# A two-layer hybrid model on one core: the order and the places of the first expert stage's weight loads

## The chip, the cores and the metric

The kernel runs on one core of a Trainium2 chip. The metric is the device time of one execution in microseconds; the time before is the median of three runs. TensorE (PE, with its weight load PEld), VectorE (DVE), ScalarE (ACT), GpSimd (POOL) and SyncE (SP) run their own instruction streams and meet at semaphores. Transfers from the device's memory run on 16 DMA engines; nearly all are issued by SyncE and go through one queue, in order.

## The reference

Two layers over T = 272 tokens (16 meta, 256 of the sequence) of width 1024. Layer 0 mixes with RWKV-7 and RG-LRU, layer 1 with gated linear attention. After each stands a mixture of experts: 32 experts in 4 groups, two chosen for each token.

```python
def hier_moe(h, w_group, b_group, w_router, b_router, w_gate, w_up, w_down):
    ...
    y = jnp.zeros_like(hf)
    for e in range(N_EXPERTS):
        hid = jax.nn.silu(hf @ w_gate[e]) * (hf @ w_up[e])
        y = y + (hid @ w_down[e]) * combine[:, e:e + 1]
    return y.reshape(B, T, D)
```

`w_gate` and `w_up` are 1024 x 256 for each expert and `w_down` is 256 x 1024, all float32: 1 MB for each matrix (here and below, 1 MB is 1024 KB), 96 MB for each layer. The part of RWKV that the text names: its output is centred head by head, scaled, gated and multiplied with the output weights.

```python
    mean = jnp.mean(o, axis=-1, keepdims=True)
    var = jnp.mean(jnp.square(o - mean), axis=-1, keepdims=True)
    o = ((o - mean) * lax.rsqrt(var + GN_EPS)).reshape(B, T, W) * ln_g.astype(f32) + ln_b.astype(f32)
```

## The kernel before, in words

Everything is written out by hand, in one program for each engine; the order of the work on an engine is the order of the lines.

**Expert stage.** `experts(y)` on TensorE goes through eight groups of four experts (q = 0 to 7). A group has three *units*, u = 3q (gate), 3q + 1 (up) and 3q + 2 (down), each of 4 MB. The tokens of each expert (at most 32) are gathered by matmuls into `xgT`, `half_gu` does gate and up (L1554, 64 matmul records of 32 x 256 for a unit), hid is turned (L1617), the down matmuls are L1630 (L1696 in the last group), and `combine` (L1512, L1514) brings the result back to the tokens. VectorE adds it to H (L2485, L2488). Between groups 3 and 4 there is a loop for experts with over 32 tokens (L1635 on), which makes one pass here.

**Places.** SBUF holds four slots of 4 MB, `slots[0]` to `slots[3]`, and `UNIT_SLOT` says which unit goes to which. In layer 0, units 0, 1, 2, 3, 4, 5 go to slots 1, 2, 3, 0, 1, 2, and unit 8 to slot 1 again. A slot may be filled once the unit before in it has been used (`wait_through`). The first units don't wait so long: parts of them have places of their own. `aside` holds the first halves (k = 0 to 3, 0.5 MB) of unit 4's up weights, for three of its four experts in layer 0; `apart` holds the first halves of unit 1's experts 1, 2 and 3. So a slot's half comes free while the other is in use, and `half_done` counts the halves used.

**Loads.** SyncE issues all of this in `experts(y)` at L348 to L486. The order around the change, for layer 0: unit 2 (down, slot 3, `whole`) after `sa_evac` 5 and `lru_in` 6; unit 0 (gate) after `oc_set` 5; unit 1 (up) after `mixE` 5, with two pieces set aside for unit 4; unit 3 (gate) and parts of unit 5 (down) after counts of `res_done` that say how much of the output projection is done; then the rest of units 4 and 5, and unit 8's halves ahead of units 6 and 7 at L441. `oc_set` is raised by VectorE for each of five chunks of the RWKV output at L2265, right after its centring; `sa_evac` is ScalarE's copy of a chunk's state, and `lru_in` 6 is the last step of the LRU (L2257). `loaded(u)` on TensorE waits for a unit's slot semaphore and, for the units in pieces, for a second one (`ld_pv_ys` for unit 1, `ld_wout` for 3, `ld_lruw_e5` for 5, `ld_u8_lastk` for 8); `ld_half` is for the pieces set aside.

**Small tiles.** `K1` holds the scan's reset mask and the GLA gate weights `gupO`; `m_lev` are masks of the RWKV stage; `wrr` are the raw router weights of both layers, turned into `wrc` by VectorE at L2303, which raises `wrc_set`. The router's scratch (`rt`) ends at column 37120 of M.

**Behind it.** Layer 1's projections (L1768, L1874), its attention, and `experts(1)`, whose loads begin at 522.30 us, when the attention's first output parts are done.

## Time and profile before

| | us |
|---|---|
| median of 3 runs | 782.89 |
| the three runs | 782.05, 782.89, 785.16 |
| span of the profiled execution | 778.7 |
| its own device time | not shown beside the runs |
| TensorE busy in the span | 718.9 (92%) |
| weight load busy | 459.4 (59%) |
| VectorE busy | 324.4 (42%) |
| mean rate of the DMA engines | 311 GB/s (242.14 MB) |
| chain that ended last: TensorE / DMA | 60% / 15% of the span |

The profile's times are from one execution, counted from its first instruction. Its own device time isn't among the numbers, so sums are made against its span. A wait is idle time of an engine and what ended it. "DMA to landing" is the time from the issue on SyncE to the last of the transfer's signals. The share of the DMA engines can come out slightly over 1.

### The profile page before, as it was taken

Reading aid. Unit: us, or ns where it says so; the run is one execution under the profiler, and the core shown is the slowest. Engines: PE = TensorE matmul, PEld = TensorE weight load, DVE = VectorE, ACT = ScalarE, POOL = GpSimd, SP = SyncE. Lnnn points to the kernel's source line nnn. Section 1 sums busy time; section 2 is a strip of 40 time slices with the busy share of each in tenths; the row PEclk is TensorE's granted clock in tenths of the full one; section 3 lists DMA queues with packets and bytes.
Section 4 is the critical chain, followed back from the end, with each engine's and each line's share of the span. In section 5 each row is a group of like instructions: output and inputs, shape, how many; then the busy total and the mean of one; then the engine's idle time right before and its main releaser. Section 6 shows DMA issues by size and latency. Waiting matters only on the chain.

```text
span 778.7 us, 16693 instructions
## 1 busy us (share of the span) xinstructions
PE 718.9 (92%) x7444; PEld 459.4 (59%) x7444; DVE 324.4 (42%) x688; ACT 205.9 (26%) x414; POOL 31.7 (4%) x99
## 2 busy tenths in 40 slices
PE   9999999999989998999999999999998976786696
PEld 7778787658646464564548746884764543343342
DVE  7476977535353422333235065541445321221222
ACT  2574577215100000000041454630510000000003
POOL 7006000000000000000000000000000000000000
PEclk9999999999999997999999999999999998989999
DMA  8644113499999999999999731019999999999995
GB/s 265 201 107 142 56 57 112 161 418 417 386 420 419 420 421 421 417 419 422 411 339 370 231 107 58 2 36 424 421 391 421 422 420 419 421 422 422 420 406 199
DMA packets 72757, 242.14 MB, mean 311 GB/s; under 512 B 9894, under 2 KB 37660, under 8 KB 52588
## 3 DMA queue, kind: packets, MB, share of 16 engines
q1 hardware_dynamic: 72476, 240.52, 79.0%
q8 instruction: 59, 0.97, 0.5%
q10 hardware_dynamic: 208, 0.54, 0.2%
q14 instruction: 14, 0.11, 0.0%
HBM read 240.00 MB, written 1.05 MB: 310 GB/s over the span
## 4 chain that ended last, share of the span: by engine, by line
PE 60%; DMA 15%; DVE 4%; issue 1%; SPq 1%; ACT 0%; ACTq 0%
PE ps L1554 11%; PE ps L1874 10%; PE ps L1396 7%; PE ps L1497 6%; DMA M<-in_m_w_gate_dram 6%; PE ps L1630 5%; PE ps L1512 5%; DMA M<-in_m_w_up_dram 4%; DMA M<-in_m_w_down_dram 4%; PE ps L1035 2%; DVE H L2488 1%; PE ps L1411 1%; PE ps L1696 1%; PE ps L1768 1%; PE ps L1505 1%
## 5 line engine op out<-in xcount | busy, mean ns | idle before, releaser
L1554 PE MATMUL ps<-M 128*32 128x256 f32 x2016 | 124.2, 396 | 18.4 <-DMA M<-in_m_w_gate_dram 11.4
L1554 PEld LDWEIGHTS ps<-M 128*32 128x32 f32 x2016 | 66.7, 114 | 74.7 <-issue 16.9
L1089 PE MATMUL ps<-M 128*128 128x272 f32 x352 | 85.3, 397 | 0.1
L1874 PE MATMUL ps<-M 128*128 128x256 f32 (+2 forms) x288 | 79.9, 434 | 0.0
L1497 PEld LDWEIGHTS ps<-M 128*128 128x128 f32 x608 | 71.5, 192 | 12.3 <-issue 11.8
L1497 PE MATMUL ps<-M 128*128 128x128 f32 x608 | 76.9, 278 | 0.0
L1089 PEld LDWEIGHTS ps<-M 128*128 128x128 f32 x352 | 65.6, 190 | 15.4 <-issue 1.7
L1630 PE MATMUL ps<-M 128*32 128x512 f32 x448 | 58.7, 671 | 15.5 <-DMA M<-in_m_w_down_dram 15.5
L1512 PE MATMUL ps<-M 128*128 128x512 f32 (+1 forms) x120 | 62.8, 647 | 5.3 <-DVE H L2488 5.3
L1874 PEld LDWEIGHTS ps<-M 128*128 128x128 f32 x288 | 53.7, 190 | 22.6 <-issue 15.6
L2485 DVE TENSOR_TENSOR H<-H,ps 128x512 f32<-128x512 f32 x60 | 41.2, 687 | 57.5 <-PE ps L1512 57.3
L1396 PE MATMUL ps<-M 128*128 128x512 f32 (+1 forms) x160 | 57.5, 512 | 0.0
L2464 DVE TENSOR_TENSOR M<-ps,gm 128x512 f32<-128x512 f32 x28 | 19.4, 692 | 59.7 <-PE ps L1497 59.7
L1512 PEld LDWEIGHTS ps<-M 128*128 128x128 f32 (+1 forms) x120 | 19.9, 194 | 40.7 <-DVE H L2485 18.1
L1630 PEld LDWEIGHTS ps<-M 128*32 128x32 f32 x448 | 15.7, 120 | 47.7 <-issue 46.5
L831 ACT ACTIVATE M<-ps 128x256 f32<-128x256 f32 x16 | 6.1, 383 | 140.7 <-PE ps L1554 140.7
L1396 PEld LDWEIGHTS ps<-M 128*128 128x128 f32 x160 | 29.6, 190 | 23.0 <-issue 21.5
L833 ACT ACTIVATE M<-ps 128x272 f32<-128x272 f32 x16 | 6.4, 397 | 127.1 <-PE ps L1505 127.1
L2540 DVE COPY M<-ps 128x512 f32<-128x512 f32 x14 | 9.7, 692 | 64.2 <-PE ps L1630 64.2
L839 ACT ACTIVATE M<-ps 128x512 f32<-128x512 f32 x16 | 9.6, 597 | 62.2 <-PE ps L1630 57.3
L2488 DVE TENSOR_TENSOR H<-H,ps 16x256 f32<-16x256 f32 x32 | 13.3, 414 | 29.7 <-PE ps L1514 29.4
L1021 POOL TENSOR_SCALAR M<-M,rs 128x512 f32<-128x512 f32 x1 | 1.6, 1566 | 548.0 <-DVE rs L1990 548.0
(462 smaller groups left out, 843.6 us busy)
## 6 DMA issues: line engine op xcount, KB each, us to landing
M<-in_m_w_gate_dram SPq DMA_DIRECT2D x31, 2048.0 KB, 19.0
M<-in_m_w_down_dram SPq DMA_DIRECT2D x24, 2048.0 KB, 22.8
M<-in_m_w_up_dram SPq DMA_DIRECT2D x24, 2048.0 KB, 21.6
M<-in_o_w_in_dram SPq DMA_DIRECT2D x12, 1024.0 KB, 9.5
M<-in_e_w_in_dram SPq DMA_DIRECT2D x11, 1024.0 KB, 6.7
M<-in_m_w_down_dram SPq DMA_DIRECT2D x10, 1024.0 KB, 18.1
M<-in_m_w_up_dram SPq DMA_DIRECT2D x9, 1024.0 KB, 17.9
M<-in_m_w_down_dram SPq DMA_DIRECT2D x4, 1536.0 KB, 13.3
```

Source lines behind the costliest of these rows:

```text
L1035: pe.matmul(ps[:, bank, :].rearrange("p (a c) -> p a c", a=4), ones[:, :], ones[:, :].unsqueeze(1).to_broadcast([P, 4, P]), start=True, st ...
L1089: ins = pe.matmul(ps[:, n % 4, 0:T], wringE[:, (n // 2) % 4, k, (n % 2) * P:(n % 2) * P + P], (xnE if n else xuE)[:, k], start=(k == 0), s ...
L1396: ins = pe.matmul(res, mixT[:, k, TOK[n]], w_out, start=(k == 0), stop=(k == 7))
L1497: ins = pe.matmul(ps[:, 1 + k // 4, (k % 4) * P:(k % 4) * P + P], xn[:, n, k, :], R[:, n, :], start=(n == 0), stop=(n == nt - 1))
L1512: return pe.matmul(ps[:, bank, :], rt_[:, TOK[n]], ys[:, 512 * hf:512 * hf + 512], start=True, stop=True)
L1554: ins = pe.matmul(ps[32 * e:32 * e + 32, 3 * x, 0:FF], xgT[q % 2][:, k, 32 * e:32 * e + 32], w, start=(k == 0), stop=(k == KD - 1))
L1630: ins = pe.matmul(ps[r, 4 + hf, :], hidT[:, k, r], dn_w[UNIT_SLOT[y][u]][:, e, k, 512 * hf:512 * hf + 512], start=(k == 0), stop=(k == 1))
L1874: ins = pe.matmul(ps[rows, unit % 4, 0:n], lhs(k), rhs(k), start=(k == 0), stop=(k == KD - 1))
L2464: return tt(xgT[q % 2][:, 4 * b:4 * b + 4], ps[:, 1 + b, :].rearrange("p (k t) -> p k t", k=4), gm[:, y, 4 * b:4 * b + 4].unsqueeze(2).to_ ...
L2485: return tt(H[:, n, c], H[:, n, c], ps[:, 6 + j % 2, :], ALU.add)
L2488: ins = tt(H[0:META, 2, c], H[0:META, 2, c], ps[32 * g:32 * g + META, 6 + j % 2, 0:256], ALU.add)
L2540: v.tensor_copy(yst[q % 2][:, 512:1024], ps[:, 5, :]).then_inc(s("yd"), 1)
```

## The change

1. `aside[0]` has a fourth place, at column 36096 of M: the first half of unit 4's expert 7 goes there as well (`set_aside(3)`), right behind unit 2. To make room, the router's scratch must end at 36096; `GE`, `DF`, `mR` and `mW` move to free columns below.
2. `apart[0]` is new: k = 0 to 2 of unit 1's expert 0, 0.375 MB, in `K1` at columns 1024 to 1792, sent after `wrc_set` 1. `K1` grows to 2112 columns and takes in `m_lev` and `wrr`, whose own tiles go.
3. Unit 2's first two experts are sent after the first `oc_set` instead of with the rest.
4. The place that (2) frees in slot 2 takes k = 0 to 2 of unit 5's expert 4, in the issues after `res_done` 5.
5. Unit 4's remaining halves go in two pieces of 1 MB after `half_done` 1. With slot 1's second halves no longer used by unit 4, all four second halves of unit 8 go after `gate_done` 1, ahead of unit 5's (before: three of them, behind unit 5's).
6. TensorE's `loaded(1)` waits for one transfer more, and `half_gu` reads the weights from the new places.

```diff
--- before.py
+++ after.py
@@ -108,14 +108,14 @@
         K0 = sb("K0", [P, 1056])
         m_ar = K0[:, 512:640].rearrange("p (x t) -> p x t", x=2)
         hsel, E2, cen, onesbd = K0[:, 640:672], K0[:, 672:800], K0[:, 800:928], K0[:, 928:1056]
-        K1 = sb("K1", [P, 1152])
+        K1 = sb("K1", [P, 2112])
         reset, gupO = K1[:, 0:640].bitcast(BF16), K1[:, 640:1152]
         ident = sb("ident", [P, P])
         ones = sb("ones", [P, P])
         id64 = sb("id64", [P, 64])
         before = sb("before", [P, P])
         iota = sb("iota", [P, P])
-        m_lev = sb("m_lev", [P, 6, L])
+        m_lev = K1[:, 1152:1536].rearrange("p (l t) -> p l t", l=6)
         pv = sb("pv", [P, NPV])
         gnT = sb("gnT", [P, 4, KD])
         gm = sb("gm", [P, 2, KD])
@@ -123,7 +123,7 @@
         omka = sb("omka", [P, 4])
         epsb = sb("epsb", [P, 2])
         dlast = sb("dlast", [P, 4, NC])
-        wrr = sb("wrr", [P, 2, KD, NG + NE])
+        wrr = K1[:, 1536:2112].rearrange("p (y k c) -> p y k c", y=2, k=KD)
         wrc = sb("wrc", [P, KD, NG + NE])
         BI = sb("BI", [P, 2, NG + NE])
         ss = sb("ss", [P, 5, 6])
@@ -277,16 +277,18 @@
         eg, ohg, sg4 = rt(3, NG), rt(3, NG), rt(3, NG)
         pe4 = rt(3, NG, 8)
         el, rk, A8, oh1, oh2, s8 = (rt(3, 8) for _ in range(6))
-        GE, DF = rt(3, 8, 8), rt(3, 8, 8)
+        GE, DF = at(28800, 3, 8, 8), at(28992, 3, 8, 8)
         AA = rt(48).bitcast(BF16).rearrange("p (t e) -> p t e", t=3)
         WT, RM = rt(3, NE), rt(3, NE)
         cnts, fl, pos, code = rt(NE), rt(2, NE), rt(64), rt(16)
         tab = rt(MAXOV + 1, 2)
-        tc2, mk, mR, mW, rme, wte = rt(2), rt(NE), rt(3, NE), rt(3, NE), rt(3), rt(3)
+        tc2, mk, rme, wte = rt(2), rt(NE), rt(3), rt(3)
+        mR, mW = at(29216, 3, NE), at(29312, 3, NE)
+        assert free[0] <= 36096
         level, cmp = at(31616, NE, 8), at(31616 + 8 * NE, 16, NE)
 
-        aside = [[K0[:, 0:D], K1[:, 0:D], yst[1]], [K0[:, 0:D], K1[:, 0:D], at(26624, D), yst[1]]]
-        apart = [None, xgT[1].rearrange("p k t -> p (k t)"), at(33792, D), yst[0]]
+        aside = [[K0[:, 0:D], K1[:, 0:D], yst[1], at(36096, D)], [K0[:, 0:D], K1[:, 0:D], at(26624, D), yst[1]]]
+        apart = [K1[:, 1024:1024 + 3 * FF], xgT[1].rearrange("p k t -> p (k t)"), at(33792, D), yst[0]]
         fnb = H[:, 2, :]
         fin = at(D, 2, D)
         ROOT_BANK = [1, 5]
@@ -364,15 +366,18 @@
 
                 def but_quarters(u, src, rest):
                     j = UNIT_SLOT[y][u]
-                    sp.dma_start(slots[j][:, 0, :], src[:, 0, :]).then_inc(s(f"ld_s{j}"), 16)
+                    sp.dma_start(slots[j][:, 0, 3 * FF:2 * D], src[:, 0, 3 * FF:2 * D]).then_inc(s(f"ld_s{j}"), 16)
                     sp.dma_start(slots[j][:, 1:3, D:2 * D], src[:, 1:3, D:2 * D]).then_inc(s(f"ld_s{j}"), 16)
                     sp.dma_start(slots[j][:, 3, D:2 * D], src[:, 3, D:2 * D]).then_inc(s(rest), 16)
                     sp.dma_start(apart[2], src[:, 2, 0:D]).then_inc(s(rest), 16)
 
                 if y == 0:
+                    sp.wait_ge(s("oc_set"), 1)
+                    sp.dma_start(slots[3][:, 0:2, :], down[:, 0:2, :]).then_inc(s("ld_s3"), 16)
                     sp.wait_ge(s("sa_evac"), NC)
                     sp.wait_ge(s("lru_in"), 6)
-                    whole(2, down[:, 0:4])
+                    sp.dma_start(slots[3][:, 2:4, :], down[:, 2:4, :]).then_inc(s("ld_s3"), 16)
+                    set_aside(3)
 
                 for u in range(NU):
                     q, kind = divmod(u, 3)
@@ -384,6 +389,8 @@
                         but_quarters(u, up[:, 0:4], "ld_pv_ys")
                         for e in range(2):
                             set_aside(e)
+                        sp.wait_ge(s("wrc_set"), 1)
+                        sp.dma_start(apart[0], up[:, 0, 0:3 * FF]).then_inc(s("ld_pv_ys"), 16)
                         continue
                     if u == 3 and y == 1:
                         for e in range(3):
@@ -402,6 +409,7 @@
                             sp.wait_ge(s("res_done"), 5)
                             sp.dma_start(slots[j][:, 2, :], gate[:, 6, :]).then_inc(s("ld_wout"), 16)
                             sp.dma_start(slots[UNIT_SLOT[y][5]][:, 1:4, 0:D], down[:, 5:8, 0:D]).then_inc(s("ld_lruw_e5"), 16)
+                            sp.dma_start(slots[UNIT_SLOT[y][5]][:, 0, 0:3 * FF], down[:, 4, 0:3 * FF]).then_inc(s("ld_lruw_e5"), 16)
                             sp.wait_ge(s("res_done"), 6)
                             sp.dma_start(apart[3], up[:, 3, 0:D]).then_inc(s("ld_pv_ys"), 16)
                             sp.dma_start(slots[j][:, 3, :], gate[:, 7, :]).then_inc(s(f"ld_s{j}"), 16)
@@ -420,10 +428,10 @@
                             set_aside(3)
                         if y == 0:
                             sp.wait_ge(s("half_done"), 1)
-                            sp.dma_start(slots[j][:, 3, 0:D], up[:, 7, 0:D]).then_inc(s("ld_half"), 16)
-                            sp.dma_start(slots[j][:, 0:3, 0:D], up[:, 4:7, D:2 * D]).then_inc(s(f"ld_s{j}"), 16)
+                            for e in (0, 2):
+                                sp.dma_start(slots[j][:, e:e + 2, 0:D], up[:, 4 + e:6 + e, D:2 * D]).then_inc(s(f"ld_s{j}"), 16)
                             wait_through(UNIT_PREV[y][u])
-                            sp.dma_start(slots[j][:, 3, D:2 * D], up[:, 7, D:2 * D]).then_inc(s(f"ld_s{j}"), 16)
+                            sp.dma_start(slots[UNIT_SLOT[y][8]][:, :, D:2 * D], down[:, 8:12, D:2 * D]).then_inc(s("ld_u8_lastk"), 16)
                             continue
                         else:
                             sp.wait_ge(s("half_done"), 3)
@@ -434,15 +442,13 @@
                     src = (gate, up, down)[kind]
                     if y == 0 and u == 5:
                         sp.wait_ge(s("half_done"), 2)
-                        sp.dma_start(slots[j][:, 0, 0:D], down[:, 4, 0:D]).then_inc(s(f"ld_s{j}"), 16)
+                        sp.dma_start(slots[j][:, 0, 3 * FF:D], down[:, 4, 3 * FF:D]).then_inc(s(f"ld_s{j}"), 16)
                         wait_through(UNIT_PREV[y][u])
-                        sp.dma_start(slots[j][:, 0:3, D:2 * D], down[:, 4:7, D:2 * D]).then_inc(s(f"ld_s{j}"), 16)
-                        sp.dma_start(slots[j][:, 3, D:2 * D], down[:, 7, D:2 * D]).then_inc(s("ld_lruw_e5"), 16)
-                        sp.dma_start(slots[UNIT_SLOT[y][8]][:, 0:3, D:2 * D], down[:, 8:11, D:2 * D]).then_inc(s("ld_u8_lastk"), 16)
+                        sp.dma_start(slots[j][:, :, D:2 * D], down[:, 4:8, D:2 * D]).then_inc(s(f"ld_s{j}"), 16)
                         continue
                     if y == 0 and u == 8:
-                        sp.dma_start(slots[j][:, 0:3, 0:D], down[:, 8:11, 0:D]).then_inc(s(f"ld_s{j}"), 16)
-                        sp.dma_start(slots[j][:, 3, :], down[:, 11, :]).then_inc(s(f"ld_s{j}"), 16)
+                        for e in (0, 2):
+                            sp.dma_start(slots[j][:, e:e + 2, 0:D], down[:, 8 + e:10 + e, 0:D]).then_inc(s(f"ld_s{j}"), 16)
                         continue
                     for h in range(1 if u == 3 else 0, 2):
                         if u == NU - 1:
@@ -1529,7 +1535,7 @@
                     j = UNIT_SLOT[y][u]
                     pe.wait_ge(s(f"ld_s{j}"), 32 * (FIRST_LAYER[j] * y + UNIT_TURN[y][u] + 1))
                     if y == 0 and u == 1:
-                        pe.wait_ge(s("ld_pv_ys"), 304)
+                        pe.wait_ge(s("ld_pv_ys"), 320)
                     elif y == 0 and u == 3:
                         pe.wait_ge(s("ld_wout"), 80)
                     elif y == 0 and u == 5:
@@ -1547,9 +1553,9 @@
                             w = gu_w[UNIT_SLOT[y][u]][:, e, k, :]
                             if u == 4 and k < KD // 2 and e < len(aside[y]):
                                 w = aside[y][e][:, FF * k:FF * k + FF]
-                            elif u == 4 and k >= KD // 2 and (e < 3 or y == 1):
+                            elif u == 4 and k >= KD // 2:
                                 w = gu_w[UNIT_SLOT[y][u]][:, e, k - KD // 2, :]
-                            elif u == 1 and y == 0 and k < KD // 2 and e:
+                            elif u == 1 and y == 0 and k < KD // 2 and (e or k < 3):
                                 w = apart[e][:, FF * k:FF * k + FF]
                             ins = pe.matmul(ps[32 * e:32 * e + 32, 3 * x, 0:FF], xgT[q % 2][:, k, 32 * e:32 * e + 32], w,
                                             start=(k == 0), stop=(k == KD - 1))
```

SyncE's stream from the first load of the expert stage on. The names are destination and source; `M` and `K` are the tiles M and K0 or K1. Before:

```order
L363 DMA M<-in_m_w_down_dram 128x2x2048 [waits lru_in,sa_evac]
L363 DMA M<-in_m_w_down_dram 128x2x2048
L468 DMA M<-in_m_w_gate_dram 128x2x2048 [waits oc_set]
L468 DMA M<-in_m_w_gate_dram 128x2x2048
L367 DMA M<-in_m_w_up_dram 128x2048 [waits mixE]
L368 DMA M<-in_m_w_up_dram 128x2x1024
L369 DMA M<-in_m_w_up_dram 128x1024
L370 DMA M<-in_m_w_up_dram 128x1024
L354 DMA K<-in_m_w_up_dram 128x1024 x2
```

and with the change:

```order
L376 DMA M<-in_m_w_down_dram 128x2x2048 [waits oc_set]
L379 DMA M<-in_m_w_down_dram 128x2x2048 [waits lru_in,sa_evac]
L356 DMA M<-in_m_w_up_dram 128x1024
L474 DMA M<-in_m_w_gate_dram 128x2x2048 [waits oc_set]
L474 DMA M<-in_m_w_gate_dram 128x2x2048
L369 DMA M<-in_m_w_up_dram 128x1280 [waits mixE]
L370 DMA M<-in_m_w_up_dram 128x2x1024
L371 DMA M<-in_m_w_up_dram 128x1024
L372 DMA M<-in_m_w_up_dram 128x1024
L356 DMA K<-in_m_w_up_dram 128x1024 x2
L393 DMA K<-in_m_w_up_dram 128x768 [waits wrc_set]
```

The first two experts of unit 2 stand under the first `oc_set`, a piece of up weights comes ahead of the gate loads, unit 1's first piece is shorter, and the rest of it stands last, under `wrc_set`.

SyncE's stream from unit 1's last piece (experts' half after `lg_done`) to the first load of unit 6. Before:

```order
L410 DMA M<-in_m_w_up_dram 128x1024 [waits lg_done]
L423 DMA M<-in_m_w_up_dram 128x1024 [waits half_done]
L424 DMA M<-in_m_w_up_dram 128x3x1024
L426 DMA M<-in_m_w_up_dram 128x1024 [waits gate_done]
L437 DMA M<-in_m_w_down_dram 128x1024 [waits half_done]
L439 DMA M<-in_m_w_down_dram 128x3x1024 [waits up_done]
L440 DMA M<-in_m_w_down_dram 128x1024
L441 DMA M<-in_m_w_down_dram 128x3x1024
L468 DMA M<-in_m_w_gate_dram 128x2x2048 [waits dn_done]
```

and with the change:

```order
L418 DMA M<-in_m_w_up_dram 128x1024 [waits lg_done]
L432 DMA M<-in_m_w_up_dram 128x2x1024 [waits half_done]
L432 DMA M<-in_m_w_up_dram 128x2x1024
L434 DMA M<-in_m_w_down_dram 128x4x1024 [waits gate_done]
L445 DMA M<-in_m_w_down_dram 128x256 [waits half_done]
L447 DMA M<-in_m_w_down_dram 128x4x1024 [waits up_done]
L474 DMA M<-in_m_w_gate_dram 128x2x2048 [waits dn_done]
L474 DMA M<-in_m_w_gate_dram 128x2x2048
```

Unit 4's remaining halves are two pieces, unit 8's four second halves stand right behind them under `gate_done`, and unit 5 has two loads left, one of 0.125 MB and one of 2 MB.

## Rows read from the trace of the kernel before

**Rows 1.** Waits of TensorE, 150 to 410 us: waiter, awaited, total us, times, longest.

```profile
PE ps L1512 <- DVE H L2488: 5.3, 7, 0.8
```

**Rows 2.** The same view, 600 to 760 us.

```profile
PE ps L1630 <- DMA M<-in_m_w_down_dram: 15.5, 4, 4.3
```

**Rows 3.** Busy times by stretch: PE, PEld, DVE, ACT, POOL, clock, DMA share, GB/s.

```profile
131.00:147.00 16.00, 14.83 (x538) 12.78 (x536) 14.33 (x28) 8.06 (x24) 0.00 (x0) 1.00 0.02 4
196.00:199.00 3.00, 2.93 (x49) 1.79 (x52) 2.57 (x13) 0.07 (x1) 0.00 (x0) 1.00 0.90 283
210.00:379.00 169.00, 158.69 (x1536) 93.01 (x1535) 60.57 (x121) 12.13 (x28) 0.53 (x1) 0.97 1.01 420
379.00:403.00 24.00, 22.77 (x203) 10.31 (x205) 7.72 (x14) 5.17 (x12) 0.00 (x0) 1.00 1.03 375
602.00:738.00 136.00, 103.78 (x1006) 55.97 (x1003) 30.05 (x50) 8.21 (x19) 0.00 (x0) 0.92 1.01 421
```

**Rows 4.** Issues and landings of L468 and L452, layer 0's group 7.

```profile
L468 SPq DMA_DIRECT2D M<-in_m_w_gate_dram x2: 367/420/472, 360.7 to 361.1; - x2
...
DMA to landing us min/median/max: 15.1/17.3/19.6
...
L452 SPq DMA_DIRECT2D M<-in_m_w_down_dram x4: 2985/4900/5281, 372.1 to 387.3; - x4
...
DMA to landing us min/median/max: 15.1/18.3/21.2
```

**Rows 5.** Timelines of weight load (PEld) and TensorE (PE): start, us, then the instructions.

```profile
198.37 3.21 PEld L1554 LDWEIGHTS ps<-M 128*32 128x32 f32 x64 [0.30 <-issue]
...
230.36 3.64 PE L1630 MATMUL ps<-M 128*32 128x512 f32 x32
...
245.68 3.18 PEld L1554 LDWEIGHTS ps<-M 128*32 128x32 f32 x64 [0.76 <-issue]
...
303.32 5.49 PE L1512 MATMUL ps<-M 32*128 32x512 f32 x6 [0.77 <-DVE H L2488]
...
317.51 3.03 PE L1512 MATMUL ps<-M 128*128 128x512 f32 x6 [0.76 <-DVE H L2488]
...
381.38 3.18 PEld L1554 LDWEIGHTS ps<-M 128*32 128x32 f32 x64 [0.76 <-DMA M<-in_m_w_gate_dram]
...
402.80 1.45 PEld L1696 LDWEIGHTS ps<-M 128*32 128x32 f32 x32 [0.17 <-issue]
```

**Rows 6.** Issues and landings of five lines, 146 to 203 us.

```profile
L363 SPq DMA_DIRECT2D M<-in_m_w_down_dram x1: 368/368/368, 146.6 to 146.6; - x1
...
DMA to landing us min/median/max: 9.0/9.0/9.0
...
L468 SPq DMA_DIRECT2D M<-in_m_w_gate_dram x2: 368/495/622, 147.9 to 148.3; - x2
...
DMA to landing us min/median/max: 17.7/19.9/22.2
...
L354 SPq DMA_DIRECT2D K<-in_m_w_up_dram x2: 432/740/1047, 160.7 to 161.1; - x2
L354 SPq DMA_DIRECT2D M<-in_m_w_up_dram x1: 432/432/432, 186.3 to 186.3; - x1
...
DMA to landing us min/median/max: 10.7/18.1/19.6
...
L440 SPq DMA_DIRECT2D M<-in_m_w_down_dram x1: 628/628/628, 202.5 to 202.5; - x1
...
DMA to landing us min/median/max: 9.8/9.8/9.8
```

**Rows 7.** Timeline of VectorE, first centring and router weights.

```profile
132.31 0.43 DVE L2265 TENSOR_TENSOR M<-M 128x256 f32<-128x256 f32 x1
...
158.70 0.45 DVE L2303 TENSOR_TENSOR wrc<-wrr,gnT 128x288 f32<-128x288 f32 x1
```

**Rows 8.** Timeline of SyncE's issues, 194 to 196 us.

```profile
195.06 0.33 SPq L423 DMA_DIRECT2D M<-in_m_w_up_dram  x1
```

## Prediction

> **What bounds the kernel now.** I read the waits first, because the change only touches loads. From the last projection of layer 0 to the end of its expert stage TensorE's waits are short and end on VectorE; no DMA ends one [rows 1]. The longest group is 5.3 us in seven waits, all for the accumulation into H. In layer 1 it is different: there `w_down` alone ends four waits of 15.5 us in total [rows 2]. So the kernel has two regimes. Up to the start of layer 1's expert loads TensorE sets the pace, and from there the transfers do.
>
> The stretches say how near the two are in layer 0 [rows 3]. Between 131 and 147 us the DMA engines move 4 GB/s, that is nothing. From 210 to 379 us they move 420 GB/s at share 1.01, while TensorE is busy for 158.69 of 169 us. Both are full. Layer 1's stage has the same 421 GB/s, but TensorE is busy for only 103.78 of 136 us. Full transfers alone therefore don't make layer 0 bound by transfers; the landings have to be set beside the moments of use.
>
> A landing is the issue time plus the delay that the view of a line gives. At the tail of layer 0's stage, unit 21 (gate of group 7) lands at 361.1 + 19.6 = 380.7 us, and its first weight load starts at 381.38. The last piece of all, issued at 387.3, lands 15.1 us later, at 402.4, and is used from 402.80 [rows 4, 5]. The margins are 0.7 and 0.4 us, with a margin in between at the other units. The trace names a DMA as what ended a 0.76 us gap of the weight loader before 381.38, but the same 0.76 us with no DMA in it stands before 245.68 [rows 5], where the transfers are far ahead. It is the rhythm of that place and no wait for data. Layer 0 is bound by TensorE, with transfers that are just in time at its end.
>
> **The change part by part.** The transfers are one queue, so I keep account in MB. A piece of 2 MB costs 4.9 us: the gate pair lands at 147.9 + 17.7 = 165.6 and 148.3 + 22.2 = 170.5 [rows 6]. That is 2.5 us for each MB, which is also what 420 GB/s gives.
>
> First, **two experts of the third unit at the first centring**. The first `oc_set` comes with the VectorE instruction that begins at 132.31 and takes 0.43 us, while the old condition let the first issue go at 146.6 [rows 6, 7]. SyncE has by then issued the last piece of `e_w_out`, and nothing else waits behind the new wait that isn't held by the later one anyway. 2 MB start at 132.8. The same 2 MB needed 9.0 us from issue to landing in an empty queue before [rows 6], so they land at 141.8, inside the idle stretch. At 147 us 6.5 MB are in the queue (2 down, 0.5 of up's new place, 4 gate) in place of 8: the gate ends 1.5 x 2.5 = 3.7 us sooner, at 166.8 instead of 170.5.
>
> Second, **the places for up weights**. Unit 1's expert 0 is cut into 0.625 and 0.375 MB. The 0.375 MB go to K1 and wait for `wrc_set`; that instruction starts at 158.70 and takes 0.45 us [rows 7], and SyncE comes to it only behind the pieces set aside, the second of which it issued at 161.1 [rows 6], so the wait is free. Unit 1's volume stays 4 MB with the two pieces set aside: landing 177.0 instead of 161.1 + 19.6 = 180.7 [rows 6]. The place so freed in slot 2 takes 0.375 MB of the second group's down weights early, 0.9 us of queue. What is left is 3.7 - 0.9 = 2.8 us at 187 us. The piece of up weights issued at 186.3 landed 10.7 us later, at 197.0 [rows 6]; the 0.5 MB behind it, the last that unit 1 waits for, therefore at 198.2, and TensorE begins unit 1 at 198.37 with no wait to speak of [rows 5]. After the change it lands at about 195.4. That saves nothing, because nothing waited.
>
> Then the queue runs dry. The next issue stands at 195.06, bound to the first half of the gate matmuls (`half_done` 1) [rows 8], which TensorE doesn't reach sooner. Before, the engines lost about 1 us there: 283 of 420 GB/s over 3 us [rows 3]. Now they lose nearly 4. From that moment the head start is only the volume already sent and not yet due before: 0.5 + 0.375 MB, x 2.5 = **2.2 us**, whatever the early 2 MB gained.
>
> Third, **the third group's down halves sooner**. 2 MB (unit 8's second halves) go at once at `gate_done` 1 in front of unit 5's 2.1 MB, where 1.5 MB went behind. From the dry moment to unit 5's last byte 6.1 MB pass in place of 5.0, so unit 5 lands 2.8 us later than its 202.5 + 9.8 = 212.3 [rows 6], at 215.1. TensorE begins it at 230.36 [rows 5]: the margin of 18 us covers it, and with that cover gone it would cost those 2.8 us. In total nothing is added: the same bytes, in one transfer more (25 for 24 up to the sixth unit). All later issues wait for slots that TensorE frees, at the same times, with a deep queue, so all landings move 2.2 us earlier: unit 21 to 378.5, the last one to 400.2.
>
> The matmuls are the same in number and shape; some read their weights from K1 or M at another place. The moved router scratch, `m_lev` and `wrr` are the same instructions on other addresses. I cost these at nothing from both sides; a price would be seen in instruction lengths, and none of the rows has a shape that changes.
>
> **Sum.** Removed from the path: 0. Added: 0. The profiled span of 778.7 would stay 778.7 +- 0.3. The median of the runs, 782.9, lies 4.2 above that span, and the runs span 3.1 us. With margins of 0.4 to 0.7 us at the tail, an execution whose transfers come half a microsecond later does wait, and the change spares it that. I take 0.3 us for it: **782.6 us**. The most that the tail can hide is four such gaps of 0.76 us, 3.0 us, if after all they were waits.
>
> The Trainium skill (DMA: Bandwidth & Descriptors, Anatomy of one DMA) speaks against this change: its fit, made on the GpSimd path, has a fixed cost of about 2 us for each DMA beside its bytes, and its section Bandwidth, Measured, advises transfers of at least 1 MiB. One transfer more would then eat 2.0 of the 2.2 us and leave the landings where they are; the sum for TensorE would still be 0. The trace doesn't agree for a queue that is full: from 170.5 to 180.7 us, 10.2 us, six transfers with 4 MB land, and 4 MB alone are 9.9 us.
>
> **The rivals.**
> *The tail was waiting.* The four or five units of group 7 follow their landings by 0.2 to 0.7 us, one after the other, which is odd for pure chance. If TensorE is held there in most executions, 2.2 us of head start returns up to 2.2 us, at most 3.0: 780.7, and 779.9 at the end. Everything behind follows, since layer 1's loads start at a moment that layer 0 sets. Against it: busy instructions stand end to end in that stretch, 22.77 of 24 us [rows 3]. Chance 0.16.
>
> *The head start isn't there, and unit 1 waits.* This is the case where the change doesn't do what it says: the early 2 MB don't get through in the gap, but the 0.875 MB are in front of unit 1 all the same. Its last piece then lands at 198.2 + 2.2 = 200.4, TensorE stands 2.0 us at 198.4, and everything behind moves by that: 784.9. It decides when the head start at 147 us is under 2.2 us instead of the 5 worked out from the idle stretch. Chance 0.06. By the same page's fixed cost it would take one extra transfer more, and the time would be up to 2 us longer still, 786.9.
>
> *The clock falls once more.* Around 303 us six combine matmuls take 5.49 us where six take 3.03 at 317, at the lower of the two levels [rows 5]: a loss of 2.5 us. It follows a stretch of short, thin matmuls. A new stall of 2 us at 198 with such a fall behind it gives 782.9 + 2.0 + 2.5 = 787.4. The 0.8 us waits of the normal groups [rows 1] bring no fall in the 169 us that run at a mean of 0.97 [rows 3], so 0.04.
>
> **How the numbers follow.** No effect has 0.74, with 781 to 784.8 from the runs shown. About half a percent, 3.9 us, is what a measurement of this kernel can tell from no change. The first rival stays within that except at its end, so faster gets 0.07, slower gets 0.06 from the last rival and part of the second, and the same 0.87. The range reaches from the first rival's end, 779.9, to past the second's 784.9: 785.4.
>
> **What would show it.** Right: a landing of unit 21 near 378.5 and of the last piece near 400.2; the first 2 MB landed by 142; a hole in the transfers before 195 to 197 us wider than before; TensorE's instructions of 150 to 403 us within 0.3 us of their old places. Wrong: expert matmuls of group 7 that begin over 1 us sooner relative to group 6, a DMA as the end of a wait at 198 us, or a different time of `oc_set`.

## The result, and the profile after

| | before | with the change |
|---|---|---|
| median | 783.06 us (6 executions) | 787.87 us (6 executions) |
| lowest, highest | 779.5, 785.16 | 787.53, 788.7 |
| span of the profiled execution | 778.7 | 786.1 (its own time 787.82) |
| ratio | | 1.0079, 95% interval 1.0063 to 1.0095 |

The changed kernel is slower. The two medians differ by 4.8 us (0.6%); the ratio on record, which is not that of the medians and which all comparisons below use, is 0.8%, 6.2 us of 783. The forecast was 782.6 and no change. The changed kernel's profiled execution took 1.7 us more than its span. If that holds for the one of before too, its 778.7 is an execution of some 780.4 (an estimate): 2.7 below its median. So the two spans differ by 7.4 us, more than the medians, and the positions below add up to those 7.4.

Nearly all of it (7.26 us) arises before 213 us. First the stretch that [rows 3] showed as 131 to 147 us, cut in three (columns as there). The kernel before:

```profile
131.00:137.50 6.50, 5.76 (x225) 4.99 (x223) 5.71 (x11) 4.05 (x12) 0.00 (x0) 1.00 0.01 3
137.50:141.00 3.50, 3.32 (x135) 2.92 (x128) 3.01 (x7) 1.51 (x5) 0.00 (x0) 1.00 0.02 5
141.00:147.00 6.00, 5.75 (x210) 4.87 (x205) 5.61 (x12) 2.50 (x8) 0.00 (x0) 1.00 0.02 5
```

and the changed kernel, with layer 0's expert stage behind it:

```profile
131.00:137.50 6.50, 5.71 (x204) 4.80 (x195) 5.68 (x11) 3.94 (x11) 0.00 (x0) 1.00 0.57 178
137.50:141.00 3.50, 0.38 (x14) 0.38 (x16) 1.28 (x3) 0.00 (x0) 0.00 (x0) 0.81 0.68 281
141.00:147.00 6.00, 5.82 (x145) 5.14 (x145) 2.55 (x6) 1.74 (x5) 0.00 (x0) 0.54 0.03 7
210.00:379.00 169.00, 158.69 (x1535) 92.95 (x1535) 60.41 (x120) 12.55 (x29) 0.53 (x1) 0.97 1.01 415
```

The middle row is the finding. While the 2 MB move (281 GB/s), TensorE is busy for 0.38 of 3.5 us and VectorE for 1.28. Then they have moved, the DMA engines are quiet again at 7 GB/s, and TensorE is busy, but with 145 matmuls where there were 210, at a granted clock of 0.54: most of the 6 us are spent at 1.2 GHz. Layer 0's expert stage answers [rows 3] to the digit, 158.69 of 169 us. Everything in it stands 7.3 us later, and nothing in it got longer.

Timeline of SyncE, TensorE and VectorE of the changed kernel (start, us, instructions, in brackets the idle time before them):

```profile
132.93 0.37 SPq L376 DMA_DIRECT2D M<-in_m_w_down_dram  x1
...
133.48 0.27 PE L1287 MATMUL ps<-M 64*64 64x64 f32 x2 [0.41 <-issue]
...
137.05 0.40 PE L1270 MATMUL ps<-M 64*64 64x64 f32 x11
140.62 0.37 PE L1270 MATMUL ps<-M 64*64 64x64 f32 x2 [3.17 <-issue]
...
143.75 0.42 DVE L2291 TENSOR_TENSOR M<-M,ps 128x256 f32<-128x256 f32 x1 [4.97 <-issue]
```

The stop is in the middle of a run: sixteen equal 64 x 64 matmul records of L1270 stand one behind the other (the kernel before runs all sixteen, from 136.79 on, without a gap). Two, then the eleven shown go, 3.17 us pass, the last three go. Nothing that the program waits for lies between the thirteenth and the fourteenth. The view calls it "issue", idle time with no releaser. So no semaphore and no data is seen to end it, which leaves that TensorE had no next instruction; the experiments test that. VectorE's 4.97 us at 143.75 are read as the same stop seen from behind.

The waits of TensorE from 100 to 620 us, those that end on issue:

```profile
PE ps L1270 <- issue: 3.2, 1, 3.2
...
PE ps L1287 <- issue: 0.4, 1, 0.4
```

The kernel before has no stop in that run of matmuls, and 0.2 us in place of the 0.4. (Both have another 0.8 us on issue at the tail of layer 0's stage.) What the instructions come by is in part 3 of the page, and was there in the page of before, with the same numbers: a queue for instructions of 59 packets, 0.97 MB, that is 16 KB for each. It must be TensorE's: its 7444 matmuls and 7444 weight loads are 252 for each packet, while VectorE has 688 instructions in all. Its traffic was the 4 GB/s of [rows 3]. The DMA view of the kernel before, 134 to 135.5 us (40 slices, then the queue: packets, MB, share of its engines):

```profile
GB/s 0 0 0 0 0 0 0 437 0 0 0 0 0 0 0 0 0 0 0 0 0 0 0 0 0 0 0 0 0 0 0 0 0 0 0 0 0 0 0 0
...
q8 instruction: 1, 0.02, 5.8%
```

One packet, in the eighth slice, at 134.27 us; the next ones are at 138.13, 141.69 and 145.27, so TensorE uses one up in about 3.6 us there. In the changed kernel the view of 131.2 to 138 us has no such packet, only the load, and the view behind it has it:

```profile
q1 hardware_dynamic: 166, 1.36, 61.0%
...
q1 hardware_dynamic: 77, 0.63, 101.2%
q8 instruction: 1, 0.02, 4.0%
```

It stands at 138.31 us. The load was issued at 132.93 and landed 9.1 us later, at 142.0. The block that was due at 134.27 came 4.0 us late, and TensorE went on at 140.62, 2.3 us behind it. It was late already while TensorE still ran at its old places (137.05 for 136.89), so the late block is not the effect of the stop. The rest of the loss follows in the chain that ended last. Before:

```profile
150.20 7.06 PE ps L1396 x16
...
187.83 2.92 PE ps L1411 x24
...
205.84 3.57 PE ps L1630 x32
```

After:

```profile
137.45 3.17 issue
...
155.97 7.06 PE ps L1402 x16
...
193.60 4.54 PE ps L1417 x24
...
213.10 3.57 PE ps L1636 x32
```

The same 16 matmuls of the output projection are 5.77 us late at 155.97. The long stop is 3.2 of it, and TensorE stood 0.2 late ahead of that, which leaves 2.4 for the low clock. Its rows say nearly the same: 145 for 210 matmuls in 6 us are 1.9 us of work not done by 147 us. Up to 188 us nothing is added (193.60 against 187.83). There 24 matmuls take 4.54 us for 2.92, a second low stretch of the clock (0.71 in 196 to 199 us), and at 213.10 the delay is 7.26 us. It is 7.4 at the end.

And the head start that the change was to give is there. Issues and landings at the tail of layer 0's stage in the changed kernel, to be set beside [rows 4, 5], and the weight loader:

```profile
L474 SPq DMA_DIRECT2D M<-in_m_w_gate_dram x2: 368/419/470, 368.0 to 368.4; - x2
...
DMA to landing us min/median/max: 13.3/15.6/17.8
...
L458 SPq DMA_DIRECT2D M<-in_m_w_down_dram x4: 2483/4028/6783, 378.4 to 393.3; - x4
...
DMA to landing us min/median/max: 14.6/19.0/20.8
```

The timeline:

```profile
388.69 3.18 PEld L1560 LDWEIGHTS ps<-M 128*32 128x32 f32 x64 [0.76 <-issue]
...
410.11 1.45 PEld L1702 LDWEIGHTS ps<-M 128*32 128x32 f32 x32 [0.17 <-issue]
```

Unit 21 lands at 368.4 + 17.8 = 386.2 and is used from 388.69, a margin of 2.5 us for 0.7. The last piece, 393.3 + 14.6 = 407.9, is used from 410.11, 2.2 for 0.4. So the transfers are 1.8 us further ahead of TensorE. The weight loader's gap stays 0.76 us, and what stands behind it is now "issue" and no DMA.

### The profile page after: what moved, and what is told of

Read it like the earlier page. It is cut to its first block, busy times and chain, and to the rows that moved or that the text cites. A ratio compares the mean times of both kernels' runs of the same rounds, so it can differ in the third digit from the quotient of the medians.

```text
span 786.1 us, 16694 instructions
## 1 busy us (share of the span) xinstructions
PE 723.0 (92%) x7444; PEld 462.9 (59%) x7444; DVE 324.4 (41%) x688; ACT 206.0 (26%) x414; POOL 32.0 (4%) x99
## 4 chain that ended last, share of the span: by engine, by line
PE 73%; DMA 15%; DVE 6%; ACT 3%; issue 2%; SPq 1%; POOL 0%; ACTq 0%; POOLq 0%
PE ps L1560 11%; PE ps L1880 10%; PE ps L1095 8%; PE ps L1402 7%; PE ps L1503 6%; DMA M<-in_m_w_gate_dram 6%; PE ps L1636 5%; PE ps L1518 4%; DMA M<-in_m_w_up_dram 4%; DMA M<-in_m_w_down_dram 4%; PE ps L1041 2%; DVE H L2494 1%; PE ps L1417 1%; PE ps L1702 1%; PE ps L1774 1%
## 5 line engine op out<-in xcount | busy, mean ns | idle before, releaser
L2494 DVE TENSOR_TENSOR H<-H,ps 16x256 f32<-16x256 f32 x32 | 13.3, 414 | 29.7 <-PE ps L1520 29.4
```

The lines of the kernel that those rows point to most:

```text
L2494: ins = tt(H[0:META, 2, c], H[0:META, 2, c], ps[32 * g:32 * g + META, 6 + j % 2, 0:256], ALU.add)
```

## The experiments

Two theories stood at the start. **A**: the block of instructions is late, since the 2 MB occupy the engines that bring it. **B**: the 2 MB write into SBUF, in rows that TensorE and VectorE are reading and writing, and hold them back there. **C** was the suspicion that the other parts of the change cost as well. The ratios are to the kernel before, with 95% intervals.

### The change without its early issue

```diff
-                    sp.wait_ge(s("oc_set"), 1)
-                    sp.dma_start(slots[3][:, 0:2, :], down[:, 0:2, :]).then_inc(s("ld_s3"), 16)
                     sp.wait_ge(s("sa_evac"), NC)
                     sp.wait_ge(s("lru_in"), 6)
+                    sp.dma_start(slots[3][:, 0:2, :], down[:, 0:2, :]).then_inc(s("ld_s3"), 16)
```

> The change without the early issue: both halves of unit 2 go together after the old condition, all else as changed. Theory A (the 2 MB sent at the first centring hold up the instruction blocks that TensorE fetches over the same DMA engines, so TensorE stands 3.2 us in the middle of a run of matmuls and its clock falls behind that): no hole at 137 to 141 us, granted clock 1.00 from 131 to 147 us, and a time of 783 us, ratio 0.998 to 1.003. Rival B (the writes into SBUF disturb the engines' reads there, whenever they come): the same as A here. Rival C (the new places, the cut pieces and the new order of the loads cost it): time stays at 786 to 788.

784.60 us for 781.72, ratio 1.0035 [1.0022, 1.0048]. The stop and the low clock are gone, as A and B said, but the time isn't back at 783. TensorE waits once at unit 1:

```profile
204.74 0.38 PE L1559 MATMUL ps<-K,M 128*32 128x256 f32 x1 [2.96 <-DMA M<-in_m_w_up_dram]
```

By stretch (columns as in [rows 3]):

```profile
137.50:141.00 3.50, 3.15 (x124) 2.78 (x116) 3.26 (x9) 1.63 (x5) 0.00 (x0) 1.00 0.02 5
```

(This execution stands 2.7 us later than that of before already at 131 us, so the window holds other instructions of the same stage. From 141 to 147 us the clock is 1.00 as well.)

This is the mechanism of the prediction's second rival, for which it priced 2.0 us: without a head start, TensorE waits 3.0 us there. Whether the 0.875 MB in front of unit 1's last piece are the reason is tested further down.

### The early issue alone, in the kernel before

```diff
                 if y == 0:
+                    sp.wait_ge(s("oc_set"), 1)
+                    sp.dma_start(slots[3][:, 0:2, :], down[:, 0:2, :]).then_inc(s("ld_s3"), 16)
                     sp.wait_ge(s("sa_evac"), NC)
                     sp.wait_ge(s("lru_in"), 6)
-                    whole(2, down[:, 0:4])
+                    sp.dma_start(slots[3][:, 2:4, :], down[:, 2:4, :]).then_inc(s("ld_s3"), 16)
```

> The kernel before with the early issue alone: first two experts of unit 2 at the first centring, nothing else changed. A and B: a hole of about 3 us in TensorE near 138 us, half clock behind it, 787 to 789 us, ratio 1.005 to 1.009. C: 783, no hole.

786.50 us for 781.72, 1.0063 [1.0047, 1.0078]. TensorE's waits (waiter, awaited, total us, times, longest):

```profile
PE ps L1266 <- issue: 2.9, 1, 2.9
PE ps L1556 <- DMA M<-in_m_w_gate_dram: 0.8, 1, 0.8
```

By stretch (columns as in [rows 3]):

```profile
137.50:141.00 3.50, 0.60 (x37) 0.47 (x34) 1.45 (x3) 0.10 (x1) 0.00 (x0) 1.00 0.66 272
141.00:147.00 6.00, 5.82 (x159) 5.22 (x153) 3.60 (x8) 1.99 (x6) 0.00 (x0) 0.56 0.03 7
```

The early issue alone brings back most of the loss: the same stop, of 2.9 us, the packet at 138.21, the clock at 0.56 behind it. C, which had no stop here, is out as the main cause. The second wait is another matter: it stands at unit 21, where the prediction saw a margin of 0.7 us. This execution has used it up, without the new places that widen it in the change, so up to 1.0 us of its loss (0.2 more at a later unit) is a wait for weights. The two kernels don't add up to the change (1.0035 and 1.0063 against 1.0079), as they need not: where the 2 MB are early, unit 1 doesn't wait.

### Where the 2 MB go: not to SBUF

In the kernel before, the same 2 MB are read at the first centring and written to a scratch tensor in the device's memory; the weights are then loaded as ever. The copy is extra work, and its result isn't used. (The program's end waits for it.)

```diff
                 if y == 0:
+                    sp.wait_ge(s("oc_set"), 1)
+                    sp.dma_start(y_dram[0:512].rearrange("(p e k) d -> p e (k d)", e=2, k=2), down[:, 0:2, :]).then_inc(s("ld_copy"), 16)
```

> The kernel before, with the same 2 MB read at the first centring but written to scratch in the device's memory instead of SBUF; unit 2 is loaded as before. Theory A (instruction blocks held up behind the transfer on the DMA engines): the instruction block comes late again, near 137 to 138.5 us instead of 134.3, and TensorE has a hole of 2 to 3 us in the same run of matmuls: 785 to 788. Rival B (the writes into SBUF disturb the engines): no hole, 782.

785.89 us for 781.57, 1.0051 [1.0033, 1.0069]. TensorE's waits, as above:

```profile
PE ps L1267 <- issue: 1.8, 1, 1.8
```

By stretch (columns as in [rows 3]):

```profile
137.50:141.00 3.50, 1.71 (x51) 1.45 (x51) 1.40 (x3) 0.38 (x1) 0.00 (x0) 0.91 0.87 351
141.00:147.00 6.00, 5.82 (x142) 5.25 (x144) 3.86 (x8) 1.74 (x5) 0.00 (x0) 0.50 0.02 5
```

Not a byte of it goes to SBUF, and TensorE stops in the same run of matmuls, for 1.8 us, with the packet at 137.05 and the clock at 0.50 behind. So a write into SBUF isn't needed for the stop. It is a little shorter than the 2 to 3 us expected. Here too TensorE waits at the tail, 1.1 us for unit 21's gate weights, so the time isn't that of the stop alone.

### Half the bytes, and the bytes in pieces

One expert (1 MB) at the first centring:

```diff
-                    sp.dma_start(slots[3][:, 0:2, :], down[:, 0:2, :]).then_inc(s("ld_s3"), 16)
+                    sp.dma_start(slots[3][:, 0, :], down[:, 0, :]).then_inc(s("ld_s3"), 16)
```

(The other 3 MB go after the old condition.)

> The change with 1 MB instead of 2 at the first centring (the other 3 MB of unit 2 after the old condition). A: the block of instructions due at 134.3 us comes 2.5 us sooner than in the change (at about 135.8 instead of 138.3), the hole shrinks from 3.2 to 0.7 us or less, the clock doesn't fall in 131 to 147 us, 783 to 784. B: half the bytes, half the disturbance, 785. C: 788.

784.43 us for 781.72, 1.0042 [1.0028, 1.0056]. The packet comes at 136.98, the stop is 2.1 us, and the clock does fall behind it (0.72). Half the bytes save a third of the stop, not all but 0.7 us as A expected, and the time is between A's 783 to 784 and B's 785.

Four pieces of 0.5 MB, one behind each centring:

```diff
-                    sp.wait_ge(s("oc_set"), 1)
-                    sp.dma_start(slots[3][:, 0:2, :], down[:, 0:2, :]).then_inc(s("ld_s3"), 16)
+                    for n in range(4):
+                        sp.wait_ge(s("oc_set"), n + 1)
+                        w = slice(D * (n % 2), D * (n % 2) + D)
+                        sp.dma_start(slots[3][:, n // 2, w], down[:, n // 2, w]).then_inc(s("ld_parts"), 16)
```

(TensorE waits for all four before unit 2, and the rest of it is loaded as before.)

> The change with its early 2 MB in four pieces of 0.5 MB, one after each of the first four centrings (132.7, 137, 141 and 144.6 us). The same bytes in the same 14 us. A: a piece holds a block of instructions up for 1.3 us at most, which the blocks fetched ahead cover: no hole, 783 or a little under. B: the same bytes, 786 to 788. C: 788.

782.89 us for 781.72, 1.0024 [1.0005, 1.0042]. A had expected no stop. Only the first piece makes one of over 0.3 us (packet at 136.47 for 134.27), and the clock stays up:

```profile
PE ps L1273 <- issue: 1.1, 1, 1.1
```

By stretch (columns as in [rows 3]):

```profile
137.50:141.00 3.50, 2.31 (x95) 1.97 (x91) 1.82 (x4) 0.65 (x2) 0.00 (x0) 1.00 0.47 154
141.00:147.00 6.00, 5.48 (x186) 4.75 (x190) 4.97 (x12) 2.73 (x9) 0.00 (x0) 1.00 0.29 90
```

### The whole 2 MB one centring later, and in shorter rows

The change with `oc_set` 2 in place of 1, so that the 2 MB go at 137.14 us, ahead of another packet:

```diff
-                    sp.wait_ge(s("oc_set"), 1)
+                    sp.wait_ge(s("oc_set"), 2)
```

> The change with its whole early 2 MB after the second centring (137 us) instead of the first (132.7). It tells the size from the place: three pieces of 0.5 MB from there on left no hole. If a transfer in one go holds a block of instructions up wherever it stands, the block due at 138.1 comes at 140 to 142 and TensorE has a hole of 1.5 to 3 us behind it, clock down: 785 to 788. If only the first place is thin, there is no hole and the time is 782.

785.62 us for 781.11, 1.0057 [1.0034, 1.0081]. The packet due at 134.27 is there at 134.62, ahead of the load, and TensorE runs through 137 to 141 us with 3.32 of 3.5 us busy. The packet that stood at 141.69 in the kernel before comes at 143.98, and the stop moves with it, with a smaller one in front:

```profile
141.50 0.27 PE L1278 MATMUL ps<-M 64*64 64x64 f32 x2 [0.49 <-issue]
...
146.40 0.30 PE L1338 MATMUL ps<-M,K 128*32 128x64 f32 x4 [1.32 <-issue]
```

By stretch (columns as in [rows 3]):

```profile
137.50:141.00 3.50, 3.32 (x122) 2.84 (x115) 3.03 (x8) 1.64 (x5) 0.00 (x0) 1.00 0.84 250
141.00:147.00 6.00, 4.01 (x146) 3.43 (x145) 3.64 (x8) 1.67 (x5) 0.00 (x0) 1.00 0.50 209
147.00:154.00 7.00, 7.00 (x116) 4.34 (x115) 2.97 (x5) 1.43 (x5) 0.00 (x0) 0.51 0.60 200
```

The matmul line is now another one (L1338), and the clock falls as it did in the change, only later: 0.51 from 147 to 154 us. So it isn't anything about L1270 and the first centring. The smaller stop at 141.50 tells something too. Its packet, due at 138.13, starts in time, at 138.29, but takes 1.8 us for the 1.0 of the kernel before, as it moves beside the load, and TensorE stops for 0.5 us. A block can be late by its end alone.

Last, the change with the first issue cut by columns, so that the rows are 2 KB long where they were 8 KB, in four transfers without a wait between them (TensorE waits for them before unit 2, and the other two experts go in two transfers):

```diff
-                    sp.dma_start(slots[3][:, 0:2, :], down[:, 0:2, :]).then_inc(s("ld_s3"), 16)
+                    for n in range(4):
+                        w = slice(512 * n, 512 * n + 512)
+                        sp.dma_start(slots[3][:, 0:2, w], down[:, 0:2, w]).then_inc(s("ld_parts"), 16)
```

> The change with its early 2 MB at the first centring in four transfers with rows of 2 KB, issued back to back, in place of one with rows of 8 KB. If the blocks of instructions wait for whole packets of the transfer that is ahead on their engine, shorter packets let them in sooner: hole well under 3.2 us (1 us or less), near the 784 of the smaller pieces. If they wait for all that was issued before them, or only the bytes count: hole of 3 us again, 787 to 788.

784.85 us for 781.11, 1.0044 [1.0029, 1.0059]. The same bytes at the same time, and the packet is in at 136.86, not at 138.31:

```profile
PE ps L1273 <- issue: 1.4, 1, 1.4
```

By stretch (columns as in [rows 3]):

```profile
137.50:141.00 3.50, 2.10 (x89) 1.83 (x85) 1.61 (x3) 0.38 (x1) 0.00 (x0) 0.99 0.98 318
141.00:147.00 6.00, 5.66 (x183) 4.97 (x175) 4.61 (x10) 2.31 (x7) 0.00 (x0) 0.72 0.06 19
```

The stop falls from 3.2 to 1.4 us. So the row size, or the cut into four, matters; the 1 us or less that was expected isn't reached. The Trainium skill (DMA: Bandwidth & Descriptors, Queues, rings and completion order) says that each engine goes round the queues that have work and drains a whole packet of one queue, about 9 to 17 descriptors, before it turns. The agreement is in direction: shorter rows let the block in 1.45 us sooner. In size it is an estimate, which takes a row (what the profile calls a packet) for a descriptor: a row of 8 KB takes 0.32 us (77 of them in 101.2% of 16 engines' 1.5 us), so 9 to 17 are 2.8 to 5.4 us, and the block was 4.0 us late. A row of 2 KB takes 0.10 us (476 in 97.6% of 16 engines' 3 us, 135.5 to 138.5), so 9 to 17 are 0.9 to 1.7 us, less than the 2.6 measured. What makes up the rest no run here shows.

### Pieces behind the later centrings, and the tail

The next form sends 1.5 MB in three pieces behind the second, third and fourth centring, and the fourth 0.5 MB at the old moment (TensorE waits for the three before unit 2):

```diff
+                    for n in range(3):
+                        sp.wait_ge(s("oc_set"), n + 2)
+                        w = slice(D * (n % 2), D * (n % 2) + D)
+                        sp.dma_start(slots[3][:, n // 2, w], down[:, n // 2, w]).then_inc(s("ld_parts"), 16)
```

> The change with 1.5 MB early, in three pieces of 0.5 MB after the centrings 2, 3 and 4 (137, 141 and 144.6 us), none at the first; the fourth 0.5 MB after the old condition. The run with four pieces had its only hole over 1 us (1.08) behind the first piece, 132.9 us. A with that place being the one where TensorE lives on its last block: no hole over 0.3 us; the head start of 3.7 us is over the 2.2 us that the new places put ahead of unit 1, so no wait for a DMA at 198 us: 781.5 to 782.5, ratio 0.999 to 1.001. If any piece of 0.5 MB costs a hole wherever it stands: 783.5.

781.71 us for 781.57, 1.0014 [0.9991, 1.0038]. From 131 to 147 us there is no stop on issue above 0.25 us, and the clock keeps its full level. Its first piece is issued at 137.36, again just ahead of a packet (due at 138.13, in at 138.81, 0.7 us late), and stops nothing; why the piece of 133 us makes its packet 2.2 us late, these runs don't tell. And unit 1 waits for up weights:

```profile
PE ps L1565 <- DMA M<-in_m_w_up_dram: 1.2, 1, 1.2
```

By stretch (columns as in [rows 3]):

```profile
141.00:147.00 6.00, 5.82 (x212) 5.06 (x208) 5.32 (x11) 2.23 (x7) 0.00 (x0) 1.00 0.44 126
```

The same with the fillers of group 7 gone, whose time a better margin at the tail should give back (`keep_busy` is dummy matmuls that keep TensorE going; they aren't part of the result):

```diff
-                        if q == NQ - 1 and y == 0:
-                            keep_busy(2, 3)
...
-                keep_busy(2, 4)
+                if y == 1:
+                    keep_busy(2, 4)
```

> As the run before it, and in layer 0 without the two fillers of group 7, four matmul records of 1.9 us each (keep_busy ahead of the last gate unit and ahead of the last down unit). If the new places bring the landings of the tail forward by 2.2 us, TensorE can use up to that: it begins unit 21 1.7 us sooner and the stage ends 2 us sooner, 779.5 to 780.5, unless the clock falls there. If the head start isn't at the tail: DMA waits take the fillers' places, 782.

783.07 us for 781.57, 1.0012 [0.9993, 1.0030]. A miss for the gain of 2 us that a head start at the tail was to give; it is the other case of the expectation, DMA waits in the fillers' place. TensorE comes sooner and waits for the last down weights, and the clock goes down there (0.84 from 390 to 400 us):

```profile
396.43 1.56 PE L1705 MATMUL ps<-M 128*32 128x512 f32 x5 [2.33 <-DMA M<-in_m_w_down_dram]
```

By stretch (columns as in [rows 3]):

```profile
390.00:400.00 10.00, 7.47 (x59) 2.96 (x58) 1.80 (x3) 2.38 (x5) 0.00 (x0) 0.84 1.06 378
```

With 1.5 MB sent early, the tail of layer 0 has no margin that could pay for the fillers. (This execution also has a low stretch of the clock at 188.5 to 192 us, 0.51, where the form with fillers has 1.00. The fillers come only 190 us later, so it isn't theirs.)

Last, the change without any early issue, with its added pieces behind unit 1's last one:

```diff
-                    set_aside(3)
...
                             sp.dma_start(apart[3], up[:, 3, 0:D]).then_inc(s("ld_pv_ys"), 16)
+                            set_aside(3)
```

(`set_aside(3)` and the 0.375 MB of unit 5 both move there, and the early issue is gone as in the first experiment.)

> The change without the early issue and with the two added pieces (0.5 MB of unit 4, 0.375 MB of unit 5) behind unit 1's last piece instead of ahead of it. In the run without the early issue TensorE waited 3.0 us for up weights before unit 1's second half... and cost 1.0035. If that wait is the 0.875 MB ahead of unit 1 (2.2 us): it is gone, 781.5 to 782.5, ratio 0.999 to 1.001. If the cut pieces or the K1 place cost it: 784.5 still.

781.83 us for 781.57, 1.0005 [0.9988, 1.0022]. At unit 1 TensorE waits 0.4 us for up weights in place of 3.0; the other 0.9 us of such waits are in group 7, at 387 and 392 us. So what cost the first experiment its time was the volume ahead of unit 1, not the places or the cut pieces.

### All the stops side by side

"Packet" is the start of the packet in the queue for instructions, "on" the first matmul behind the stop. Each row is read from one traced execution.

| kernel | sent at | load | packet | stop, us | on | on - packet |
|---|---|---|---|---|---|---|
| before | | | 134.27 | none | | |
| three pieces | 137 on | 0.5 MB each | 134.63 | none | | |
| four pieces | 133 | 0.5 MB | 136.47 | 1.08 | 138.65 | 2.2 |
| 2 KB rows | 133 | 2 MB | 136.86 | 1.40 | 139.18 | 2.3 |
| to device memory | 133 | 2 MB | 137.05 | 1.79 | 139.37 | 2.3 |
| one expert | 133 | 1 MB | 136.98 | 2.08 | 139.35 | 2.4 |
| early issue alone | 133 | 2 MB | 138.21 | 2.90 | 140.53 | 2.3 |
| the change | 133 | 2 MB | 138.31 | 3.17 | 140.62 | 2.3 |
| second centring | 137 | 2 MB | 143.98 | 1.32 | 146.40 | 2.4 |

Seven kernels with very different loads stop, and in each TensorE goes on 2.2 to 2.4 us behind the packet's start, which is 1.2 to 1.4 us behind its end. The small stops keep to the same: the 0.49 us above end 1.4 us behind the end of their packet, and so do the 0.2 us that the kernel before has at 133.15 (packet at 130.70, 1.1 us long). The stop is the packet's lateness less 0.6 to 1.2 us, whether it was due at 134.27 or, in the last row, at 141.69. The stop doesn't follow the bytes, the place they go to or the line that it falls in. This is what shows A, and it leaves nothing for B: the copy that stays out of SBUF obeys the same sum as the loads.

## Why the prediction was wrong

**What bounds the kernel** held. TensorE sets the pace to the end of layer 0's stage, and the margins at the tail were rhythm and no waits: unit 21's margin opened from 0.7 to 2.5 us and the 0.76 us stayed. The first rival, that the tail was waiting, is therefore out for the traced execution. That other executions wait there isn't excluded: the early issue alone, the copy and the late places show 0.9 to 1.4 us of such waits in group 7, and the forms with the places and an early load, fillers kept, show none. But no version shows a gain from it, and no run shows the 0.3 us that the forecast took off for it. The run without fillers adds what the prediction only touched: the tail is so near to the transfers that time taken off TensorE there comes back as a wait.

**"2 MB start at 132.8 ... so they land at 141.8, inside the idle stretch"** is the step that failed. As a transfer it was right to 0.2 us (132.93, landed at 142.0). As a cost it was wrong. I read 4 GB/s as "nothing" and priced a load in an idle stretch at zero, while these 4 GB/s were the one traffic that TensorE can't do without: 16 KB in each 3.6 us. Its sum, "Removed from the path: 0. Added: 0", lacks a term of 3.2 us for the stop, one of 2.4 us for the clock behind it, and one of 1.5 us for the second low stretch at 194 us (7.26 at 213.10 less 5.77). That the last one comes from the stop isn't shown.

**What hides it elsewhere**: from 150 us on the instruction packets of the kernel before stand at 151.9, 178.2, 195.8, 204.0 and 216.7. The DMA engines are full there, but a block of large matmuls lasts 8 to 26 us, and no stop on issue shows. That a delay of 4 us would be covered there is an argument; how late those packets were, no run shows. In the stretch of 64 x 64 matmuls a block lasts 3.6 us, so a delay counts, and the kernel before had no loads in it.

**Head start**: worked out as 2.2 us at the tail, measured as 1.8. The stop took some of the start away: the first loads behind the old condition go at 152.41 us in place of 146.62, and until then the engines stand nearly still. The dry queue before the first half of the gate matmuls is there too, ahead of the issue at 202.38, which was at 195.06 before: the engines are down to 33 GB/s where they fell no lower than 225 in any microsecond of that place before. The third part of the change held as well: unit 5's last byte lands at 209.38 + 13.3 = 222.7 us and is used from 237.69, a margin of 15 us for 18. The second row below is the second low stretch of the clock. By stretch, the changed kernel:

```profile
147.00:152.00 5.00, 4.82 (x193) 4.27 (x184) 4.29 (x9) 2.02 (x6) 0.00 (x0) 1.00 0.01 3
196.00:199.00 3.00, 3.00 (x22) 2.80 (x20) 0.99 (x7) 0.65 (x3) 0.00 (x0) 0.71 1.00 410
201.00:203.00 2.00, 2.00 (x33) 1.37 (x23) 0.53 (x4) 1.32 (x2) 0.00 (x0) 1.00 0.09 33
```

**Second rival** (unit 1 waits): its mechanism exists, 3.0 us in the first experiment for the 2.0 priced, but not in the change, where the 2 MB were early enough. Its time, 784.9, is met by that experiment's 784.6.

**Third rival** (a stall and then the clock): the right pair with the wrong cause and at the wrong place. A stall of 2 us and 2.5 us of clock made 787.4; the measured median is 787.87. That the two are so near is partly luck: its 4.5 us stand against 7.1 us of stop and clock in the traces, which differ by more than the medians do. The price of the clock, 2.5 us for a low stretch [rows 5], was a fair one, with 2.4 and 1.5 measured.

**Range and chances**: 785.4 and 0.06 for slower were too narrow, because all rivals priced data (which weights are late) and none an engine's own supply. Of everything the change did, only the 2 MB were new work for a stretch in which something else ran at its limit, and that stretch was looked at for its rate alone.

Whether the clock falls, and for how long, isn't settled by the length of the stop alone. With stops of 2.9 and 3.2 us it is granted 0.54 to 0.56 in 141 to 147 us, with 1.8 us (to device memory) 0.50, with 2.1 and 1.4 us (one expert, 2 KB rows) 0.72, with 1.1 us 1.00; behind the second centring's 0.5 and 1.3 us it is 0.51 from 147 to 154 us. Why it falls a second time, at 192 to 194 us, in the change, in the one-expert form and with 2 KB rows, and not with the early issue alone (granted 1.00 from 192 to 198 us), is open. A low stretch of that kind also stands at 188.5 us in the run without fillers, which has no stop, so a stop isn't needed for it.

## What to carry to other kernels

A stretch in which the DMA engines show a few GB/s isn't free: look which queue these bytes belong to. If it is the instructions of an engine that runs many short matmuls (here a 16 KB block in 3.6 us), a bulk load sent there stops that engine in mid-run, with "issue" as the releaser, and the clock may go down behind it (here in six of the seven kernels that stopped for over 1 us); send it in small pieces (0.5 MB behind the later centrings stopped nothing here), or wait for a stretch with long instructions. And before a load is sent sooner, ask which wait it ends: here none did, so there was nothing to win against the risk.

## What the runs showed that I had not expected

- **TensorE starves for instructions behind a load.** A 16 KB block comes 2.2 to 4.0 us late behind 0.5 to 2 MB, and TensorE goes on 2.2 to 2.4 us after the packet's start. The Trainium skill (Runtime: NRT & Kernel Launch, Instruction fetch mechanics) describes a FIFO refilled in blocks of 16 KiB by the sequencer's own DMA queue while it executes, and calls the fetch hidden. The blocks agree with that (0.97 MB in 59 packets). That it is hidden nearly holds in the kernel before, with one stop of 0.2 us in this stretch, and not behind a load, with stops of 1.1 to 3.2 us.
- **The delay isn't proportional to the bytes.** 0.5, 1 and 2 MB sent at 133 us give stops of 1.1, 2.1 and 2.9 to 3.2 us. The same 2 MB give 1.4 us in 2 KB rows, and 1.8 us from memory to memory. What else sets it is open.
- **A transfer's 16 shares don't land together.** In the three-piece form unit 1's last wait is for one late share; the first and the last signal of most transfers stand about 4.4 us apart there, and 1.9 to 2.0 in the kernel before. So 1.2 us of wait came where the account in MB had left a margin. Why one engine lags was not tried.
- **None of the versions beats the kernel before.** The best, the late places without an early issue and the three pieces with and without fillers, have intervals that include 1.
